# Two transformer blocks on one Trainium2 core: rings of banks, weight splits and the memory norm of the first block

## The reference, cut to what matters

```python
def first_block(x, mem, ...):                  # x: 512 tokens x 1024, mem: 256 x 1024, DEPTH = 2
    for l in range(DEPTH):
        h = rms_norm(x, ln_mix[l])
        x = x + parallel_mixer(h, w_in[l], ...)          # GQA and MLA heads beside each other, then w_o
        h = rms_norm(x, ln_mem[l])
        x = x + memory_cross_attention(h, rms_norm(mem, ln_mem_kv[l]), w_mem_q[l], w_mem_kv[l], w_mem_o[l])
        h = rms_norm(x, ln_ffn[l])
        x = x + expert_choice_moe(h, w_router[l], w_gate[l], w_up[l], w_down[l])
    return rms_norm(x, ln_final)

# in parallel_mixer: proj = h @ w_in; q, k heads = apply_rope(rms_norm(.)); two latents are normed and
# projected again; two softmax attentions; merged = [rms_norm(o_g), rms_norm(o_m)]; merged @ w_o
```

## Time and profile before

| | |
|---|---|
| three runs | median 3454.47 us (3450.35 to 3457.32) |
| the profiled execution | 3454.83 us, its span 3453.0, mean granted clock 0.955 |
| PE, PEld | busy 3139.2 (91%), 2179.6 (63%) |
| DVE, ACT, POOL | busy 1357.0 (39%), 1068.1 (31%), 234.5 (7%) |
| DMA | 414.25 MB, mean 120 GB/s |

### The profile page before, as it was taken

One profiled execution on the slowest core, in us unless ns is written; L12 is line 12 of the kernel. 1 busy time (PEld: TensorE's weight loads), 2 busy tenths in 40 slices (PEclk: granted clock), 3 DMA queues, 4 the chain that ended last, 5 costly groups with the idle time before them and its releaser, 6 DMA issues.

```text
span 3453.0 us, 40577 instructions
## 1 busy us (share of the span) xinstructions
PE 3139.2 (91%) x16400; PEld 2179.6 (63%) x16400; DVE 1357.0 (39%) x2122; ACT 1068.1 (31%) x1836; POOL 234.5 (7%) x318
## 2 busy tenths in 40 slices
PE   6899979996899979997999977999999999879998
PEld 4557844444657844542667565888788567648886
DVE  4554541125564532122224365233333233554444
ACT  3464411113454411113213154232223312443332
POOL 1010000001010000000000231000000000300000
PEclk8899989998899989998999999999999999989999
DMA  3001138881011148886221100233221121102220
GB/s 146 27 25 57 68 130 347 363 338 71 25 38 50 72 171 342 358 361 262 77 80 53 40 11 33 103 121 122 105 115 65 75 98 59 37 25 98 98 98 37
DMA packets 61495, 414.25 MB, mean 120 GB/s; under 512 B 6992, under 2 KB 7504, under 8 KB 13696
## 3 DMA queue, kind: packets, MB, share of 16 engines
q1 hardware_dynamic: 55664, 392.59, 29.2%
q0 software_dynamic: 4496, 16.98, 1.5%
q10 hardware_dynamic: 1152, 2.10, 0.2%
HBM read 409.53 MB, written 2.10 MB: 119 GB/s over the span
## 4 chain that ended last, share of the span: by engine, by line
PE 84%; DVE 8%; ACT 3%; issue 2%; DMA 2%; POOL 1%; DVEq 0%; ACTq 0%; SPq 0%; POOLq 0%
PE banks L708 81%; DVE arena L1951 4%; PE banks L709 3%; ACT arena L1396 2%; DMA weight<-in_w_up 1%; DVE weight_part L2040 1%; ACT weight_part L1396 1%; DVE arena L2497 1%; DVE x L1951 1%; DMA weight<-in_ada_w 1%; POOL arena L2601 0%; DVE arena L2211 0%; DVE tokens_low L1951 0%; DVE arena L2209 0%; DVE arena L2229 0%
## 5 line engine op out<-in xcount | busy, mean ns | idle before, releaser
L1396 ACT ACTIVATE arena<-banks 128x512 f32<-128x512 f32 (+4 forms) x594 | 329.6, 564 | 1416.9 <-PE banks L708 1220.8
L708 PE MATMUL banks<-weight,arena 128*64 128x512 f32 (+4 forms) x2680 | 565.8, 549 | 29.3 <-ACT arena L1396 9.7
L708 PE MATMUL banks<-arena 128*64 128x128 f32 (+3 forms) x3456 | 462.6, 320 | 21.5 <-DVE arena L2229 11.8
L708 PE MATMUL banks<-arena,weight 128*128 128x512 f32 (+2 forms) x1152 | 439.0, 537 | 32.8 <-DVE arena L1951 20.1
L708 PEld LDWEIGHTS banks<-weight,arena 128*64 128x64 f32 (+2 forms) x2680 | 254.8, 146 | 307.5 <-issue 264.6
L708 PE MATMUL banks<-hidden,weight_part 128*128 128x512 f32 (+1 forms) x2304 | 446.3, 355 | 0.0
L708 PE MATMUL banks<-tokens_high,weight_part 128*128 128x512 f32 (+1 forms) x1536 | 418.5, 358 | 23.0 <-DVE tokens_low L1951 22.8
L708 PEld LDWEIGHTS banks<-hidden,weight_part 128*128 128x128 f32 x2304 | 381.1, 189 | 70.1 <-DVE arena L1951 3.5
L708 PEld LDWEIGHTS banks<-arena 128*64 128x64 f32 (+2 forms) x3456 | 318.6, 166 | 135.9 <-issue 99.7
L708 PEld LDWEIGHTS banks<-arena,weight 128*128 128x128 f32 (+1 forms) x1152 | 214.2, 190 | 238.2 <-issue 207.4
L708 PEld LDWEIGHTS banks<-tokens_high,weight_part 128*128 128x128 f32 x1536 | 275.0, 190 | 81.8 <-DVE tokens_low L1951 29.6
(11 more groups left out here) (164 smaller groups left out, 2808.5 us busy)
## 6 DMA issues: line engine op xcount, KB each, us to landing
weight<-in_w_gate SPq DMA_DIRECT2D x64, 1024.0 KB, 13.7
weight<-in_w_up SPq DMA_DIRECT2D x64, 1024.0 KB, 6.9
weight<-in_w_down SPq DMA_DIRECT2D x64, 1024.0 KB, 10.1
weight<-in_w_ff SPq DMA_DIRECT2D x64, 1024.0 KB, 4.8
weight<-in_ada_w SPq DMA_DIRECT2D x48, 1024.0 KB, 7.2
weight<-in_w_in SPq DMA_DIRECT2D x28, 1024.0 KB, 5.1
weight<-in_w_o SPq DMA_DIRECT2D x8, 1024.0 KB, 4.8
weight<-in_w_mem_kv SPq DMA_DIRECT2D x8, 1024.0 KB, 6.0
```

Of the source, the lines that this page charges most:

```text
L708: mm = lambda o, a, b, first=True, last=True: eng.matmul(o, a, b, start=first, stop=last, skip_group_check=True)
L1396: act = lambda o, i, f=ACT.Copy, **k: eng.activation(o, i, f, **k)
```

## The change

- `HIGH_SLOTS` has three slots instead of two, and five slots instead of six take loads where weights are split.
- The sums of the query, key and latent norms and the rotations take PO instead of PB. ScalarE's root and VectorE's Newton step and rope read them there.
- `joint3` multiplies all high parts of a group first, then all low weight parts.
- w_in: block 0 is split before the stage's meeting of the engines (layer 0) or at the end of the experts of layer 0 (layer 1; on VectorE ahead of the last `combine`); blocks 1 and 2 right behind the rounding of the input; later ones follow, with the root ahead of the split on ScalarE.
- w_o 2 is split in round 8 of the attention (VectorE: round 9). The splits beside the output product are then w_o 3, w_mkv 0, 1, 2. The later ones move up likewise, w_mo 0 ahead of memory attention and w_mo 1 into its round 4 (5).
- Output product: the joint group has two tiles instead of four, and the sums of the memory norm come behind it. ScalarE makes the root of the MLA outputs and rounds them before it squares the memory. VectorE adds the first two tiles to X before the memory norm.

The diff, with context left out:

```diff
@@ -463,7 +463,7 @@
-        HIGH_SLOTS = (4, 5)
+        HIGH_SLOTS = (5, 6, 7)
@@ -675,12 +675,12 @@
-                    for k in ks:
-                        if needs_high:
-                            eng.wait_ge(*after(needs_high[k]))
-                        for t in range(len(keys)):
-                            mm(o[t], lhs[t][k][0], rhs[k][0], k == 0, False)
-                            mm(o[t], lhs[t][k][1], rhs[k][0], False, False)
+                    for part in range(2):
+                        for k in ks:
+                            if needs_high and not part:
+                                eng.wait_ge(*after(needs_high[k]))
+                            for t in range(len(keys)):
+                                mm(o[t], lhs[t][k][part], rhs[k][0], k == 0 and not part, False)
@@ -842,11 +842,11 @@
-                    norm_sum(("g", l, t), S, 0, 1, "head64", ring=PB)
+                    norm_sum(("g", l, t), S, 0, 1, "head64")
...
-                    tile(("rot", l, t), [mat("rot_gqa")], [S["QN"].get(("g", l, t))])
+                    tile(("rot", l, t), [mat("rot_gqa")], [S["QN"].get(("g", l, t))], ring=PO)
@@ -870,9 +870,9 @@
-                norm_sums(("cq", l), S, range(2), 2, "one256", ring=PB)
+                norm_sums(("cq", l), S, range(2), 2, "one256")
...
-                norm_sums(("ckv", l), S, range(1), 1, "one128", ring=PB)
+                norm_sums(("ckv", l), S, range(1), 1, "one128")
@@ -923,14 +923,13 @@
-                norm_sums(("mn", l), S, range(KD), KD, "one1024", CT, PB)
...
-                w = [halves(p, j) for p in [weight_parts(("w_o", l, i)) for i in range(2)] for j in range(2)]
-                joint3([("wo", l, m) for m in range(4)], w, OP, [range(4), range(4, KD)], T, [("onh", l, k) for k in range(KD)],
-                       [("onl", l, k) for k in range(KD)], [(WF(("w_o", l, m // 2)),) if m % 2 else () for m in range(4)])
-                norm_sums(nxt, S, range(2), KD, "one1024")
-                for m in range(4, KD):
+                w = weight_parts(("w_o", l, 0))
+                joint3([("wo", l, m) for m in range(2)], [halves(w, j) for j in range(2)], OP, [range(4), range(4, KD)], T, [("onh", l, k) for k in range(KD)],
+                       [("onl", l, k) for k in range(KD)], [(), (WF(("w_o", l, 0)),)])
+                norm_sums(("mn", l), S, range(KD), KD, "one1024", CT, PB)
+                for m in range(2, KD):
@@ -1493,9 +1492,10 @@
+                if l == 0:
+                    split_high(("w_in", 0, 0))
...
-                split_high(("w_in", l, 0))
@@ -1503,28 +1503,28 @@
+                split_high(("w_in", l, 2))
...
+                    if t >= 1:
+                        root(("g", l, t - 1), S)
...
-                        split_high(("w_in", l, 2 + t // 2))
-                    if t >= 1:
-                        root(("g", l, t - 1), S, PB)
+                        split_high(("w_in", l, 3 + t // 2))
...
-                split_high(("w_in", l, 4))
-                root(("g", l, 4), S, PB)
+                root(("g", l, 4), S)
+                split_high(("w_o", l, 0))
...
-                split_high(("w_o", l, 0))
...
-                root(("cq", l), S, PB)
-                root(("ckv", l), S, PB)
+                root(("cq", l), S)
+                root(("ckv", l), S)
@@ -1559,21 +1559,21 @@
-                    if i == 4:
-                        split_high(("w_o", l, 1))
+                    if i in (4, 8):
+                        split_high(("w_o", l, i // 4))
...
+                root(("om", l), S)
+                round_outputs(1)
...
-                root(("om", l), S)
...
-                round_outputs(1)
...
-                rest = [("w_o", l, 2), ("w_o", l, 3), ("w_mkv", l, 0), ("w_mkv", l, 1)]
+                rest = [("w_o", l, 3), ("w_mkv", l, 0), ("w_mkv", l, 1), ("w_mkv", l, 2)]
@@ -1588,28 +1588,26 @@
-                    if m % 2:
-                        split_high(("w_mkv", l, 2 + m // 2))
...
+                        split_high(("w_mkv", l, 3))
...
+                split_high(("w_mq", l, 0))
...
-                    split_high(("w_mq", l, i))
+                    split_high((("w_mq", l, 1), ("w_mo", l, 0))[i])
...
-                    if m % 2:
-                        split_high(("w_mo", l, m // 2))
...
-                              lambda i: round_mem(i // TB - 2) if i >= 2 * TB + 2 and i % TB == 2 else None, 2, 4)
+                              lambda i: split_high(("w_mo", l, 1)) if i == TB else round_mem(i // TB - 2) if i >= 2 * TB + 2 and i % TB == 2 else None, 2, 4)
@@ -1668,6 +1666,8 @@
+                if l == 0:
+                    split_high(("w_in", 1, 0))
@@ -2051,13 +2051,15 @@
+                if l == 0:
+                    split_low(("w_in", 0, 0))
...
-                split_low(("w_in", l, 0))
...
+                split_low(("w_in", l, 2))
@@ -2065,13 +2067,13 @@
-                          ring=PB, frees=[(PB.free(("raw", l, t)),)])
+                          frees=[(PB.free(("raw", l, t)),)])
...
-                    tt(S["TBB"], PB.get(key), S["TAB"][:, 1, :], MUL).then_inc(*done(PB.free(key)))
+                    tt(S["TBB"], PO.get(key), S["TAB"][:, 1, :], MUL).then_inc(*done(PO.free(key)))
@@ -2082,21 +2084,20 @@
+                    gqa_norm(t)
...
-                        split_low(("w_in", l, 1 + t // 2))
-                    gqa_norm(t)
+                        split_low(("w_in", l, 2 + t // 2))
...
-                split_low(("w_in", l, 4))
...
+                split_low(("w_o", l, 0))
...
-                split_low(("w_o", l, 0))
...
-                      lambda k: (("cqn", l),) if k else (), ring=PB, frees=[(PB.free(("cq", l, j)),) for j in range(2)])
+                      lambda k: (("cqn", l),) if k else (), frees=[(PB.free(("cq", l, j)),) for j in range(2)])
...
-                      ring=PB, frees=[(PB.free(("ckv", l)),)])
+                      frees=[(PB.free(("ckv", l)),)])
@@ -2131,8 +2132,8 @@
-                    if i == 5:
-                        split_low(("w_o", l, 1))
+                    if i in (5, 9):
+                        split_low(("w_o", l, i // 4))
@@ -2140,37 +2141,38 @@
+                for m in range(2):
+                    add_x(("mix", l), m, ("wo", l, m))
...
-                rest = [("w_o", l, 2), ("w_o", l, 3), ("w_mkv", l, 0), ("w_mkv", l, 1)]
+                rest = [("w_o", l, 3), ("w_mkv", l, 0), ("w_mkv", l, 1), ("w_mkv", l, 2)]
...
-                    add_x(("mix", l), m, ("wo", l, m))
+                    if m >= 2:
+                        add_x(("mix", l), m, ("wo", l, m))
...
-                split_low(("w_mkv", l, 2))
+                split_low(("w_mkv", l, 3))
...
-                split_low(("w_mkv", l, 3))
...
+                split_low(("w_mo", l, 0))
...
-                for i in range(2):
-                    split_low(("w_mo", l, i))
...
-                              lambda i: low_mem(i // TB - 2) if i >= 2 * TB + 3 and i % TB == 3 else None, 2, 4)
+                              lambda i: split_low(("w_mo", l, 1)) if i == TB + 1 else low_mem(i // TB - 2) if i >= 2 * TB + 3 and i % TB == 3 else None, 2, 4)
@@ -2296,6 +2298,8 @@
+                if l == 0:
+                    split_low(("w_in", 1, 0))
```

## The result

| | before | after |
|---|---|---|
| median of four runs | 3455.11 us (3450.35 to 3457.32) | 3371.09 us (3367.26 to 3372.8) |
| ratio | | 0.9757, 95% interval 0.974 to 0.9774 |
| span of the profiled execution | 3453.0 | 3365.5 |

The change saves 84.0 us by the medians, where the prediction had summed up 79.2 and given 3376. The two profiled spans lie 87.5 apart: the profiled execution of the changed kernel is the fastest of its four.

The account below looks back on a forecast made before the run. TensorE, busy 91% of the span, was taken to be held by the ring of six banks. Terms of 41.3 us in layer 0 and 37.9 in layer 1, together 79.2, gave 3376 us, range 3362 to 3400.

Parts of the forecast that it names:

- Projection, 26.8: Projection: with sums and rotations in the output banks TensorE no longer waits, 57.0 us, 26.8 won a layer.
- Rival 2: Projection: banks were not the limit, TensorE waits as long at the sums; 3430 us, chance 0.06.
- Start of layer 0, 1.9: Start of layer 0: w_in 0's split runs under the sums, so root and Newton start 1.9 us earlier.
- Start of layer 1, -1.5: Start of layer 1: splits delay GpSimd's adds, 4.3 us lost; 2.8 won back at the root; net -1.5.
- Attention, -2.0: Attention: splitting w_o 2 in rounds 8 and 9 costs 2.0 us a layer, the middle of 0 and 4.2.
- The slack of 0.4: Attention round 8: ScalarE's second exponential ends at 159.5, TensorE's transposes follow at 159.87, so slack is 0.4 us.
- rival 4: More won than counted in attention, joint pair, memory attention and layer 1's start; 3361.5 us, chance 0.05.
- Output product, 11.4: Output product, memory keys and values: waits for w_o 2 and w_mkv 2 go, with slow tiles behind; 11.4 us a layer.
- Memory attention, 3.2: Memory attention: w_mo 1's split inside the rounds wins 3.7 us and loses 0.5; 3.2 a layer (0 to 4.5).
- Five raw slots and joint order, nothing: Weight loads with five slots instead of six, and the joint pair's new order of the same 48 matmuls: nothing.
- Rival 3: Block 2's feed-forward stages: five raw slots starve TensorE over 64 blocks; 3504 us at 2 us each, chance 0.03.
- Rival 1: Projection: the wait moves into the two output banks, 8 us a layer; 3395 us, chance 0.14.

Follow-up runs that it names:

- the banks alone: Kernel before with one edit, the projection's sums and rotations in the two output banks (PO); splits, slots and output stage as before: 3412.26 us, ratio 0.9879.
- three waits mended: Changed kernel, VectorE passing layer 0's meeting before splitting w_in 0, layer 1's w_in 0 split later, attention's first maxima ahead of ckv norm and key rotation: 3358.76 us.
- The doubled split: Changed kernel with ScalarE's split of w_o 2 in attention round 8 made twice: 3378.59 us, ratio 0.9779.
- the stage undone: Changed kernel with memory sums first, four joint tiles and the output stage's splits where they were before: 3394.76 us, ratio 0.9823.
- the split is undone: Changed kernel with w_mo 1 split ahead of memory attention again, w_mo 0 left where the change put it: 3380.91 us, ratio 0.9787.
- the split order back: Changed kernel with w_in 2, 3 and 4 split where they were, ahead of root and gain step, new rings kept: 3378.22 us, ratio 0.9786.

## Why the prediction was right, and where it wasn't

The forecast of 3376 was 4.9 us above the median. By its own steps:

**Projection, 26.8: right in size and mechanism.** 27.4 and 28.1 were won, and the rings are the cause. The 57.0 us from the joint pair's end to the first scores became 56.7 (38.76 to 95.45) with no wait on line 1951, and rotation 2 lost 0.4 where 0.4 was worked out. What the working didn't say is how the parts share it: the banks give 25, the earlier splits some 2 on top. Rival 2 is refuted by the ratio of 0.9879 for the banks alone. The Trainium skill, TensorE: Matmul & The Clock Gate, section HAM oscillation, reports its finding, that double-buffering in PSUM gave no further gain, for a loop of few rows that had waited for DMA; it does not carry over to this kernel, whose waits were for a bank.

**Start of layer 0, 1.9: wrong, though 1.6 were won.** The step "root and Newton start 1.9 earlier" failed. ScalarE's root does not wait for its own split only; it stands behind the stage's meeting, and VectorE passes that after its split of 2.29. Here are TensorE's sums, first before, with ScalarE's root, then after, with VectorE's split, which the root (20.60, shown above) waits for:

```profile
9.78 9.66 PE L708 MATMUL banks<-arena,mats 128*128 128x512 f32 x16 [9.78 <-DMA mats<-in_k_mats]
...
21.29 0.67 ACT L1396 ACTIVATE arena<-banks,vec 128x512 f32<-128x512 f32 x1
```

```profile
9.61 8.56 PE L708 MATMUL banks<-arena,mats 128*128 128x512 f32 x16 [9.61 <-DMA mats<-in_k_mats]
...
18.23 2.29 DVE L2040 TENSOR_TENSOR weight_part<-weight,weight_part 128x2048 fp32r<-128x2048 f32 x1 [11.92 <-ACT weight_part L1395]
```

The root started 1.85 after the end of the sums before, and 2.43 after it in the changed kernel (18.17 to 20.60). The Newton step came 4.29 after the sums before and 3.92 now, so 0.4 were won. The other 1.3 of the 1.6 in the table are the sums themselves, 16 records of the same instructions that took 9.66 us in one profile and 8.56 in the other, and began 0.2 earlier; they are not part of the change (the last section shows what differs). That 1.6 lies so near to 1.9 is luck. The run with three waits mended shows what the step left behind, 1.6 more.

**Start of layer 1, -1.5: right** (-1.6), and mending it gave 3.9. The timelines of the changed kernel there:

```profile
733.50 1.91 ACT L1395 ACTIVATE weight_part<-weight 128x2048 fp32r<-128x2048 f32 x1
...
735.44 2.29 DVE L2040 TENSOR_TENSOR weight_part<-weight,weight_part 128x2048 fp32r<-128x2048 f32 x1 [10.19 <-ACT weight_part L1395]
...
739.74 7.97 POOL L2605 TENSOR_TENSOR arena<-arena 128x512 f32<-128x512 f32 x6 [336.25 <-ACT arena L1395]
...
747.77 3.78 PE L708 MATMUL banks<-arena,mats 128*128 128x512 f32 x4 [7.41 <-POOL arena L2605]
```

The two splits stand ahead of the additions, and GpSimd starts at 739.74, which is 39.0 us earlier than before, where the last scatter is 43.0 earlier: 4.0 lost, of 4.3 worked out. The root and the Newton step, freed of the splits between them and the sums, gave 2.3 back, of 2.8.

**Attention, -2.0: wrong, and the term was 0** (0.2 and 0.4 won). The slack of 0.4 was read as the time between an exponential's end and the transposes. That left out ScalarE's own idle time of 1.0 earlier in the round, and that only half of the transposes need the second exponential. The doubled split measures the slack at about one split. That was part of rival 4.

**Output product, 11.4: right in size** (11.1 from the sums to the last query tile), and the stage undone brings back 23.7 for two layers by the medians, 22.2 by the traces. The credit was laid to the splits alone; for w_o 2 the joint group of two would have done it too.

**Memory attention, 3.2: right mechanism, too small.** 4.1 were won in layer 0, and 4.6 and 4.4 come back when the split is undone. The first transposes wait 0.35 where 0.7 was worked out, and the later rounds wait 2.0 where 0.5 was put in. What the working left out is the clock: 1.00 against 0.87 in this stage wins those waits back.

**Five raw slots and joint order, nothing: right**, at 1.0002 for the slots; for the joint order nothing shows (13.36 against 13.33 us, the median 2.5 higher with overlapping intervals). Rival 3 is refuted.

**Rival 1** (the wait moves into the output banks) showed nowhere but in the 0.4.

**The sum.** Span against span, 79.2 were forecast and 87.5 measured. The 8.3 between them are attention 4.6, the projection 1.9 (most of it in layer 1), output product and memory attention together 1.3, the rest 0.9, less 0.4 at the two starts, all for both layers. By the medians it is 84.0, since the profiled execution of the changed kernel is the fastest of its four.

## What to carry to other kernels

When the same wait repeats at equal distances and its releaser is the step that frees a buffer, count the rings first: giving the short-lived results (sums, rotations) banks of their own won 25 of 28 us a layer, and the one new order of the other engines that was tried won 1 without them. A slack is the idle time of the whole round on both engines (here about 1.8 us where 0.4 was read), not the distance between one end and one start; and a step that is "moved under other work" must be followed through every meeting of the engines that its neighbours pass. Where two edits each cure the same wait, undo them one at a time and together, or the credit goes to the wrong one.

## What the runs showed of the hardware

Where a wait comes in the middle of dense work it costs more than its length, 1.4 to 2.1 times in these runs: 15.7 us of waits in the projection cost 26 (the trace, joint pair to first scores) to 28 (the medians, a layer), the wait of 1.77 in attention cost 3.7 to 3.8, and the 8.1 us of two waits in the output stage cost 11.1. Moving the wait of 4.55 in memory attention won 4.4 to 4.6, though small waits took half its place. In the first, second and last of these the mean granted clock of the stretch lies between its two levels (0.83, 0.89, 0.87), where the same stretch without the wait has 1.00.

Not every wait costs that. Behind the wait of 2.05 in attention the eight sums took 3.70 us in 25 of 28 places (two layers of fourteen traces), and 5.32 to 5.40 in three: both layers with the banks alone, and layer 0 with the split order back. I found nothing in the traces that tells these apart but what TensorE had done earlier; why is open. With the banks alone slow stretches like these took back 9 of the 50 us won.

The first 16 sums of the program took between 8.56 and 10.10 us in the fourteen traces. The rows show a granted clock of 1.00 there, before (9.80 to 19.40) and after (9.60 to 18.20), but the single records don't agree with it. TensorE's weight loads for these sums in the kernel before:

```profile
12.51 0.34 PEld L708 LDWEIGHTS banks<-arena,mats 128*128 128x128 f32 x1 [0.52 <-issue]
13.36 0.34 PEld L708 LDWEIGHTS banks<-arena,mats 128*128 128x128 f32 x1 [0.51 <-issue]
...
15.41 0.19 PEld L708 LDWEIGHTS banks<-arena,mats 128*128 128x128 f32 x1 [0.24 <-issue]
15.84 0.19 PEld L708 LDWEIGHTS banks<-arena,mats 128*128 128x128 f32 x1 [0.24 <-issue]
```

They come 0.85 us apart at first and 0.43 apart later: half the rate, then the full one. The full rate begins at about 15.0 there and at about 12.9 in the changed kernel, and those slower sums are the 1.1 us between the two. So a clock of 1.00 that a row shows for the first microseconds of a program is not to be trusted, and a time of one profile at the start is good to 1.5 us only.
